# Experts' w1 and w3 read with features 8 p + t in tile t (runs of 4 KB instead of 2 KB), the tokens' rows permuted likewise

## The reference, cut to what matters

```
t = h.reshape(B * S, D)                       # 256 x 1024
# each token: softmax over 4 groups, best group, top 2 of its 8 experts -> comb (256 x 32)
for e in range(32):
    hid = silu(t @ w1[e]) * (t @ w3[e])       # w1, w3: 1024 x 512 each
    y = y + comb[:, e:e+1] * (hid @ w2[e])    # w2: 512 x 1024
```

## Time and profile before

| | us |
|---|---|
| median of 3 runs | 1522.9 |
| lowest, highest | 1517.42, 1524.58 |
| the profiled execution's own time | 1524.56 |
| its span (first to last instruction) | 1522.8 |

### The profile page before, as it was taken

The page is one execution under the profiler, slowest core; times in us unless marked ns, Lnnn a source line. Parts: engine busy times, 40 slices in busy tenths (PEclk is TensorE's granted clock), DMA queues, the critical chain, the costliest instruction groups (busy, mean ns, idle before and its releaser), DMA issues.

```text
span 1522.8 us, 20505 instructions
## 1 busy us (share of the span) xinstructions
PE 1248.3 (82%) x8742; PEld 970.9 (64%) x8742; DVE 676.4 (44%) x1137; ACT 454.5 (30%) x647; POOL 1.9 (0%) x15
## 2 busy tenths in 40 slices
PE   6889988698676566566757669999999989899998
PEld 3679987587432131221212149989998879899986
DVE  2546985453300000000000055355567777667975
ACT  1533341533100000000000044343444544455453
POOL 0000000000000000000000000000000000000000
PEclk8899989899697887987778689989999989999999
DMA  9686730587999999999999947444346334445652
GB/s 356 240 281 216 220 99 1 198 279 263 391 394 398 387 398 391 395 398 388 399 389 396 396 158 229 152 139 124 126 128 191 112 111 152 136 142 174 200 206 85
DMA packets 226568, 374.51 MB, mean 246 GB/s; under 512 B 8854, under 2 KB 121896, under 8 KB 226344
## 3 DMA queue, kind: packets, MB, share of 16 engines
q1 hardware_dynamic: 226304, 369.58, 68.6%
q0 software_dynamic: 144, 3.54, 0.7%
q10 hardware_dynamic: 24, 0.03, 0.0%
HBM read 372.03 MB, written 4.62 MB: 247 GB/s over the span
## 4 chain that ended last, share of the span: by engine, by line
PE 50%; SPq 22%; DVE 13%; DMA 8%; ACT 3%; issue 3%; DVEq 0%; ACTq 0%
PE bank L554 30%; SPq L2463 22%; DVE arena L1162 5%; DMA arena<-in_w 4%; PE bank L1131 4%; DVE fine L1154 4%; DMA above<-in_w 2%; DVE arena L1154 2%; PE bank L825 2%; ACT fine L1912 2%; DMA arena<-in_w_ada 2%; PE bank L551 2%; PE bank L582 1%; ACT arena L1912 1%; PE bank L751 1%
## 5 line engine op out<-in xcount | busy, mean ns | idle before, releaser
L554 PE MATMUL bank<-fine 128*128 128x256 f32 x4656 | 587.5, 289 | 34.9 <-DVE fine L1154 24.2
L554 PEld LDWEIGHTS bank<-fine 128*128 128x128 f32 x4656 | 577.6, 197 | 44.3 <-issue 33.9
L1154 DVE TENSOR_TENSOR fine<-arena,fine 128x1024 fp32r<-128x1024 f32 (+1 forms) x257 | 299.3, 1192 | 175.3 <-ACT fine L1912 165.9
L1912 ACT ACTIVATE fine<-arena 128x1024 fp32r<-128x1024 f32 (+2 forms) x279 | 267.0, 984 | 178.7 <-PE bank L554 106.7
L1912 ACT ACTIVATE arena<-bank 128x256 f32<-128x256 f32 (+2 forms) x161 | 73.5, 482 | 606.7 <-PE bank L836 194.2
L825 PE MATMUL bank<-arena 128*32 128x512 f32 x640 | 105.7, 798 | 76.0 <-DMA arena<-in_w 76.0
L1154 DVE TENSOR_TENSOR arena<-arena,bank 128x512 f32<-128x512 f32 x8 | 5.5, 689 | 299.6 <-PE bank L825 299.6
L825 PEld LDWEIGHTS bank<-arena 128*32 128x32 f32 x640 | 20.6, 129 | 154.8 <-DMA arena<-in_w 103.1
L1912 ACT ACTIVATE arena<-arena 128x512 f32<-128x512 f32 (+6 forms) x94 | 63.3, 702 | 171.1 <-DVE arena L1154 80.4
L1162 DVE SCALAR_TENSOR_TENSOR arena<-arena 128x256 f32<-128x256 f32 (+2 forms) x265 | 108.3, 481 | 1.2 <-ACT arena L1912 0.8
L825 PE MATMUL bank<-above,arena 128*32 128x512 f32 x384 | 61.7, 778 | 39.5 <-DMA above<-in_w 39.5
(11 more groups left out here) (160 smaller groups left out, 814.0 us busy)
## 6 DMA issues: line engine op xcount, KB each, us to landing
arena<-in_w SPq DMA_DIRECT2D x240, 512.0 KB, 11.7
above<-in_w SPq DMA_DIRECT2D x144, 512.0 KB, 11.4
arena<-in_w_in SPq DMA_DIRECT2D x62, 1024.0 KB, 5.3
arena<-in_w_ada SPq DMA_DIRECT2D x24, 1024.0 KB, 7.7
arena<-in_ffn_w_up SPq DMA_DIRECT2D x22, 1024.0 KB, 5.1
arena<-in_ffn_w_down SPq DMA_DIRECT2D x11, 1024.0 KB, 4.9
arena<-in_w_ada_f SPq DMA_DIRECT2D x8, 1024.0 KB, 10.6
arena<-in_w_gla_o SPq DMA_DIRECT2D x4, 1024.0 KB, 8.5
```

Source lines behind the costliest of these rows:

```text
L554: ins = e.matmul(o, w[:, k, j * P:j * P + P], x[:, kt, :], start=start, stop=stop, skip_group_check=True)
L1154: return e.tensor_tensor(o, a, b, f)
L1912: return e.activation(o, i, f, bias=bias, scale=scale)
```

## The change

w1 and w3 are viewed with `(p t)` in place of `(t p)`: tile t, partition p is now row 8 p + t of the expert's matrix and no longer row 128 t + p. A DMA takes tiles at, at + 1 of one expert: for each partition that was two runs of 512 floats (2 KB) that lay 256 KB apart, and is now 1024 adjoining floats (4 KB), with 16 KB from one partition to the next. Destination and size are the same. w2 keeps its view.

So that tile t of the tokens has the same features, ScalarE's copies write uT permuted: feature 8 p + t goes to column 128 t + p. For bank (tc, g), whose column is 8 a + t, that is `[t, 64 g + a]`: the copy reads the bank as 8 groups of 64 elements with a step of 8, and writes 8 runs of 64 elements. The diff also adds blank lines, left out here.

```diff
-        w1v, w3v, w2v = (T[n][0].rearrange("(j e) (t p) n -> j p e t n", e=4, p=P) for n in ("w1", "w3", "w2"))
+        w1v, w3v = (T[n][0].rearrange("(j e) (p t) n -> j p e t n", e=4, p=P) for n in ("w1", "w3"))
+        w2v = T["w2"][0].rearrange("(j e) (t p) n -> j p e t n", e=4, p=P)
...
             for tc in range(2):
                 for g in range(2):
                     e.wait_ge(*u_turned[tc, g])
-                    act(uT[:, tc, 512 * g:512 * g + 512], bank_of(uT_out, (tc, g))[:, :], ACT.Copy).then_inc(*uT_out.up((tc, g)))
+                    act(shaped(uT[:, tc, :], 8, P)[:, :, 64 * g:64 * g + 64],
+                        bank_of(uT_out, (tc, g))[:, :].rearrange("p (a t) -> p t a", t=8), ACT.Copy).then_inc(*uT_out.up((tc, g)))
```

## The result

| | before | changed |
|---|---|---|
| median of the runs, us | 1523.7 (4) | 1504.8 (4) |
| lowest, highest | 1517.4, 1524.6 | 1502.2, 1506.2 |
| ratio, with its 95% interval | | 0.988 (0.985 to 0.991) |
| the profiled execution's own time, span | 1524.6, 1522.8 | 1504.1, 1502.3 |

What follows compares the result with a forecast made beforehand. The experts' stage was taken as bound by its DMA loads, not TensorE or SyncE. Savings of 0.3 + 16.3 = 16.6 us off 1524.6 gave 1508.0, a median of about 1506.5; own range 1501 to 1511, chance 0.70.

Steps and rivals of the forecast that it cites:

- The price of a run: DMA engine time in the experts' loads: a straight line, some 9.3 ns per run and 37.7 ns per KB.
- 56 slots at 0.29 us: w1 and w3 slots after the first eight, in a stream without a gap: 0.29 us saved each, 16.3 us.
- The first eight slots: w1/w3 slots filling the buffers at the stage's start: down 2.3 us sooner, of which only 0.3 us survive.
- only 0.3 us of these 2.3 survive: First eight slots finish 2.3 us sooner, but the engines then wait for PE to release the ninth slot's buffer.
- The hole: Dip in the DMA rate near 409 to 411 us, engines waiting from 408.7 to 410.7 for the ninth slot.
- The copies at nothing: ScalarE's four permuted uT copies before the routing: still 0.60 us each, cost 0; rival at four times, 6.4 us, chance 0.04.
- Everything behind moves with the stage: After the last w2 slot: the next loads are tied to the products' end, so all behind moves along.
- the granted clock: Rival: PE or its clock takes back half, some 8 us of L554 and norms lost, 1515 us; chance 0.04.
- Place in memory: Rivals on w1/w3 addresses 16 KB apart: gain only partly from run length (0.06), or memory answers more slowly (0.08).
- part only: Rival: half of w2's lead comes from its unbroken block in memory; 8 us left, 1515 us; chance 0.06.
- the slower side: Rival: memory answers w1/w3's 16 KB pattern more slowly; at 348 GB/s +39 us, near 1562 us; chance 0.08.
- The Trainium skill's rule on large pitches: Cited for the slower rival: copies lost up to half their rate as partition pitch rose from 512 KiB to 4 MiB.

Runs made afterwards that it cites:

- the experiment: Changed kernel with the DMAs of the first eight slots each split into two of 256 KB, in 2 KB runs: 1506.9 us.
- the 2 KB runs apart: Changed kernel with a slot taking tiles th and th + 4, so 2 KB runs with partitions 16 KB apart: 1523.8 us, 1.0005 of the kernel before.

## Why the prediction was right

**The price of a run: right, and it carries further than I used it.** Worked from 348, 387 and 409 GB/s; the longer runs are points that it had not seen.

| contiguous run | GB/s | engine time per run, ns | 9.3 + 37.7 per KB |
|---|---|---|---|
| 1 KB | 348 | 47.1 | 47.0 |
| 2 KB | 387 | 84.7 | 84.7 |
| 4 KB | 409 | 160.2 | 160.1 |
| 8 KB | 421 | 311.3 | 310.9 |
| 16 KB | 428 | 612.5 | 612.5 |

The Trainium skill's rule, three bus cycles for each packet beside one per 32 bytes ("DMA: Bandwidth & Descriptors", section on why small descriptors are slow), would have given 2.2% from 2 KB to 4 KB. The runs gave 5.4% (387 to 409), so for runs of these lengths the two terms named give too small a difference.

**56 slots at 0.29 us: right.** The part of the stage behind the ninth slot's issue fell from 473.09 to 455.57, by 17.5 us. With 0.6 us for the first eight slots taken off, 16.9 are left, 0.30 a slot; with the whole 1.35 of the experiment on them it would be 0.289. The forecast said 0.29 and 16.3.

**The first eight slots: right in the mechanism, mis-sized.** The step "only 0.3 us of these 2.3 survive" measured about 0.6, with 1.35 as the upper bound that the experiment gives. The hole is where it was forecast, but 1.6 us long and not 2.0, and 2.3 less 1.6 leaves 0.7, which agrees.

**The copies at nothing: right**, 0.60 us each in the changed kernel and in the run with the copies only. The reason given was loose: ScalarE's rate per element isn't the same whatever the shape (in the kernel before 379 ns for 128x256 from a bank, 592 for 128x512).

**Everything behind moves with the stage: wrong by 3.9 us in the profile, by luck in the right direction.** I had put the granted clock among the rivals as a loss only. It was a gain against the profile of before, whose rest happened to be of the slower kind; the delayed changed kernel, at 616.17, shows that the same block can come out the other way. The medians differ by 18.8 us, which lies between the 17.5 of the stage and the 20.5 of the two spans; a mixture of both kinds in the unprofiled runs would do that, but their traces aren't there to show it. So of the agreement between 16.6 forecast and 18.8 measured the stage's 17.5 is the mechanism, and what lies beyond it isn't.

**The rivals.** Place in memory fell both as "part only" and as the slower side (the 2 KB runs apart). The runs were joined (packets). The Trainium skill's rule on large pitches, weighed as the slower side, found no counterpart: at 16 KB from partition to partition the trace shows 408 GB/s, and no load read here has a larger one than the 24 KB of w_ada (387 GB/s with 2 KB runs), so nothing here bears on the pitches that the rule names.

## What to carry to other kernels

Where a stage is bound by its loads and the DMA engines are busy throughout, fit a line through the engine time per contiguous run (16 engines x bytes / rate) from the windows that the trace already has; here it priced runs up to four times as long as any it was fitted on, and a permutation of the reduced dimension gave them at no cost. Then look at the two ends of the stage: what a longer run gains in the middle, a coarser release of the first buffer and more products behind the last load take back; here long runs in the middle and short ones at both ends kept most of both (1484.9 us). Before a few microseconds in an unchanged part are given to an edit, delay that part by two or three microseconds in both kernels, with more than one profile of each, and see whether they flip.

## What I had not expected

With a delay of 2.1 us ahead of it the block behind the experts took 5.1 us longer in the changed kernel, and with one of 3.0 us it took 3.6 us less in the kernel before (615.01 to 611.41 us). In both pairs TensorE's granted clock stepped between its two levels (1.2 and 2.4 GHz) at other places. A sum of terms that ends in "the rest moves along" has in this kernel an uncertainty of some 5 us from that alone.
